# Layer 0's first projections: values ended ahead of keys, evacuations in order of need, another bank for the third unit

## The reference

```python
hx = modulate(rmsnorm(x_lat, g_attn[l]), sh1x, sc1x)
hc = modulate(rmsnorm(x_ctx, g_attn[l]), sh1c, sc1c)
aqx, akx, avx, bqx, bkx, bvx = split_cols(hx @ w_in[l])
aqc, akc, avc, bqc, bkc, bvc = split_cols(hc @ w_in[l])
qx, kx, vx = gqa_heads(aqx, akx, avx, g_qa[l], g_ka[l])   # per-head RMS norm of q and k
qx, kx = apply_rope(qx, cos, sin), apply_rope(kx, cos, sin)
```

## Time and profile before

| | before |
|---|---|
| three runs, us | 1725.15, 1731.41, 1724.01 (median 1725.15) |
| the profiled execution, us | 1729.36 |
| its span, us | 1727.6 |
| mean granted TensorE clock | 0.987 |
| busy share of the span | PE 95%, PE weight load 81%, DVE 64%, ACT 45%, POOL 36% |
| chain that ended last, by engine | PE 81%, DVE 9%, issue 4%, ACT 3%, POOL 2%, DMA 1% |

### The profile page before, as it was taken

One profiled execution on the slowest core, in us unless ns is written; L12 is line 12 of the kernel. 1 busy time (PEld: TensorE's weight loads), 2 busy tenths in 40 slices (PEclk: granted clock), 3 DMA queues, 4 the chain that ended last, 5 costly groups with the idle time before them and its releaser, 6 DMA issues.

```text
span 1727.6 us, 25951 instructions
## 1 busy us (share of the span) xinstructions
PE 1647.1 (95%) x9530; PEld 1395.6 (81%) x9530; DVE 1113.2 (64%) x1744; ACT 770.1 (45%) x1273; POOL 620.5 (36%) x316
## 2 busy tenths in 40 slices
PE   5899999889999999999999998999989999999997
PEld 3778887668888888888888876788767888888886
DVE  7877678868976576676245774778665763353256
ACT  6546666554443312332133344676564543243242
POOL 0356661110132233333332307664222254444442
PEclk9899999999999999999999999999999999999999
DMA  9430000025233343443334422001103133333232
GB/s 395 174 107 25 26 25 25 16 95 192 66 109 99 108 134 99 134 124 131 134 110 134 146 98 86 25 26 38 37 25 110 62 110 98 98 97 98 98 96 87
DMA packets 45533, 168.24 MB, mean 97 GB/s; under 512 B 4736, under 2 KB 6784, under 8 KB 43520
## 3 DMA queue, kind: packets, MB, share of 16 engines
q1 hardware_dynamic: 40896, 156.50, 27.2%
q10 hardware_dynamic: 4544, 10.49, 1.7%
HBM read 161.73 MB, written 5.24 MB: 97 GB/s over the span
## 4 chain that ended last, share of the span: by engine, by line
PE 81%; DVE 9%; issue 4%; ACT 3%; POOL 2%; DMA 1%; SPq 0%; DVEq 0%; ACTq 0%; POOLq 0%
PE ps L1270 23%; PE ps L1271 22%; PE ps L1272 22%; PE ps L1401 4%; PE ps L1415 4%; PE ps L1434 2%; PE ps L1435 1%; DVE junk_lead L2145 1%; DVE sqsum L2233 1%; DVE ht L2260 1%; DMA ada_first<-first_d 1%; DVE nb L2427 1%; DVE junk_mid L2163 1%; DMA w_raw<-w_d 1%; DVE pt_lo L2452 1%
## 5 line engine op out<-in xcount | busy, mean ns | idle before, releaser
L1146 POOL TENSOR_TENSOR w_lo<-w_raw,w_hi 128x1024 fp32r<-128x1024 f32 x175 | 441.6, 2526 | 927.8 <-ACT w_hi L1718 895.4
L1270 PE MATMUL ps<-h_hi,w_hi 128*128 128x512 f32 (+1 forms) x1592 | 568.9, 357 | 11.3 <-DVE h_lo L2268 8.3
L1271 PE MATMUL ps<-h_lo,w_hi 128*128 128x512 f32 (+1 forms) x1592 | 557.3, 350 | 0.0
L1272 PE MATMUL ps<-h_hi,w_lo 128*128 128x512 f32 (+1 forms) x1592 | 557.0, 350 | 0.0
L1270 PEld LDWEIGHTS ps<-h_hi,w_hi 128*128 128x128 f32 x1592 | 303.5, 191 | 60.2 <-issue 21.0
L1272 PEld LDWEIGHTS ps<-h_hi,w_lo 128*128 128x128 f32 x1592 | 303.0, 190 | 39.8
L1271 PEld LDWEIGHTS ps<-h_lo,w_hi 128*128 128x128 f32 x1592 | 303.6, 191 | 35.5
L1718 ACT ACTIVATE w_hi<-w_raw 128x1024 fp32r<-128x1024 f32 x188 | 198.4, 1056 | 232.3 <-PE ps L1272 213.8
L1270 PE MATMUL ps<-a_hi,w_hi 128*128 128x512 f32 (+1 forms) x552 | 191.6, 347 | 1.2 <-DVE a_lo L2642 1.2
L1271 PE MATMUL ps<-a_lo,w_hi 128*128 128x512 f32 (+1 forms) x552 | 191.3, 347 | 0.0
L1272 PE MATMUL ps<-a_hi,w_lo 128*128 128x512 f32 (+1 forms) x552 | 191.0, 346 | 0.0
(11 more groups left out here) (186 smaller groups left out, 2403.5 us busy)
## 6 DMA issues: line engine op xcount, KB each, us to landing
w_raw<-w_d SPq DMA_DIRECT2D x188, 512.0 KB, 3.5
ada_b<-ada_d SPq DMA_DIRECT2D x56, 512.0 KB, 4.4
ada_first<-first_d SPq DMA_DIRECT2D x8, 1024.0 KB, 20.2
ada_lead<-ada_d SPq DMA_DIRECT2D x14, 512.0 KB, 3.7
ada_mid<-ada_d SPq DMA_DIRECT2D x10, 512.0 KB, 8.7
x_sb<-x_d SPq DMA_DIRECT2D x2, 1536.0 KB, 8.8
x_sb<-x_d ACTq DMA_DIRECT2D x1, 3072.0 KB, 11.4
x_spill_d<-x_sb ACTq DMA_DIRECT2D x1, 2048.0 KB, 7.4
```

Of the source, the lines that this page charges most:

```text
L1146: nc.gpsimd.tensor_tensor(w_lo[:, c % RING, :], w_raw[:, c % RAW, :], w_hi[:, c % RING, :].bitcast(f32), ALU.subtract).then_inc(w_lo_done, 1)
L1270: nc.tensor.matmul(out, lh, rh, start=first, stop=False)
L1271: nc.tensor.matmul(out, lh, rl_, start=False, stop=False)
L1272: return nc.tensor.matmul(out, ll, rh, start=False, stop=last)
```

## The change

Four things, all in layer 0:

1. In the last slice (k 7) of the first two units PE takes unit 1 (values) ahead of unit 0 (keys). The list `first` is turned round accordingly, so that counts 1 and 2 of `proj_done` are the values' and 3 and 4 the keys'.
2. `unit_banks`: unit 2 goes to banks 2 and 0 (before 0 and 1), unit 3 to 1 and 2, unit 4 to 0 and 1, units 5 and 6 to 2 and 0. The values' turn goes through bank 1 (before bank 2).
3. `first_out` gives the six operations that read the first two units fixed places ahead of everything else on ACT: EV of the values' g 0, EV and SQ of the keys' g 0, EV of the values' g 1, EV and SQ of the keys' g 1.
4. The planner runs with this and gives other orders on ACT, POOL and DVE. PE's and SP's orders are as before but for the last slice and the banks.

```diff
@@ unit_banks
-        return {0: (0, 1), 1: (2, 3), 2: (0, 1), 3: (2, 0), 4: (1, 2), 5: (0, 1), 6: (0, 1)}.get(u, (7, 7))
+        return {0: (0, 1), 1: (2, 3), 2: (2, 0), 3: (1, 2), 4: (0, 1), 5: (2, 0), 6: (2, 0)}.get(u, (7, 7))
@@ mixing_plan
+    def first_out():
+
+        k, v = units[:FIRST_TILES]
+        for n, x in enumerate((v["EV"][0], k["EV"][0], k["SQ"][0], v["EV"][1], k["EV"][1], k["SQ"][1])):
+            x["pos"] = -30 + .1 * n
+
...
+    if l == 0:
+        first_out()
...
-    turn_values(v0, (2, 2) if l == 0 else (2, 3), 0)
+    turn_values(v0, (1, 1) if l == 0 else (2, 3), 0)
...
-    first = [p for x in units[:FIRST_TILES] for p in x["P"]]
+    first = [p for x in units[:FIRST_TILES][::-1] for p in x["P"]]
@@ first_tiles
-                    for y in units:
+                    for y in units[::-1] if k == KT - 1 else units:
```

## The result

The change made the kernel slower, clearly though by little: 1733.51 us in the median of 20 runs (1730.42 to 1735.91) against 1727.97 us in 20 runs of before (1723.64 to 1732.16), ratio 1.0029, 95% interval 1.0021 to 1.0036. That is 5.5 us more, where 1.9 us less was forecast, and above the range of 1719.8 to 1728.4. Of the 10.2 us between the forecast 1723.3 and the measured median, 2.8 lie in before itself, whose first three runs had a median of 1725.15. By the bound of 0.5% the ratio counts as no change. The profiled execution took 1732.62 us, its span is 1730.8 us, its mean clock 0.986.

What follows compares the result with a forecast made beforehand. It took DVE, not PE, to end the stretch near the start: PE gains 3.69 us, DVE only 1.60 + 0.27 = 1.87, the other terms nothing. So 1725.15 becomes 1723.3 us (0.11% faster), range 1719.8 to 1728.4.

Steps and rivals of the forecast that it cites:

- Pause and fall at 65 to 72 us: PE at unit 2's start: the pause goes (1.97 us) and the clock's fall at 68 us with it (1.72 us).
- The first shuffle: DVE's shuffle of the keys, forecast to start at 65.96 instead of 66.23, a gain of 0.27 us.
- the second at 74.23: DVE's shuffle of unit 2, forecast at 74.33 instead of 76.20, with the 1.60 us wait ahead of it gone.
- Unit 6's weights late on ACT: Raw load lands at 75.9, ACT stands 1.3 us; PE loses some 0.7 us, covered by its idle time at the turn.
- DVE, not PE, is what ends this stretch: From 76.2 to 105.1 us DVE is on the path, so PE's 3.69 us gain counts only as DVE's 1.87.
- the term for DVE: DVE up to the values' low part: gains 1.60 + 0.27 = 1.87 us, whatever PE gains.
- the shuffle of unit 3, now ahead of ada tile 23: DVE's new order was to change no time there, only needing unit 3's evacuation one tile sooner, at 82.9 us.
- Its low part: DVE's low part of the values' first piece, forecast to start at 102.43 instead of 104.30.
- that the gain reaches the end of the program: Rest of units 5 and 6, head factors and everything that follows were all to move by 1.87 us.
- one fall of the clock more or less: Allowance in the range for a short fall elsewhere in the program, 1.7 us each way.
- the idle time at the turn: PE waiting for DVE before the values' second piece: 1.6 to 2.3 us in place of 0.48.
- The second rival: The clock's fall moves to the values' turn, costing 1.72 us: -0.15 us in all, 1725.0 us; chance 0.20.

Runs made afterwards that it cites:

- p_act: The change with only ACT's fixed order (keys first); banks, turn's bank and last slice as before; 1727.23 us, ratio 0.9994 against before.
- a_gate: The change with the gate's two small DVE additions planned behind ada tile 29 instead of tile 23; 1727.91 us, ratio 1.0002 against before.
- b_hit: The kernel before with only the gate's additions moved, behind ada tile 24 instead of 23, onto POOL's split; 1734.93 us, ratio 1.0036 against before.
- a_both: The change with the gate's additions behind ada tile 29 and the values' first low part ahead of tiles 28 and 29; 1724.51 us, ratio 0.9981.
- after_3: The change itself, unaltered, timed once more against before on the same chip; 1733.27 us, ratio 1.0029.
- a_vl: The change with DVE taking the values' first low part ahead of ada tiles 28 and 29; 1725.76 us, ratio 0.9987 against before.
- both edits: Gate's additions behind ada tile 29, values' first low part ahead of tiles 28 and 29; ratios 0.9981 (change), 1.0002 (before), 0.9985 (ACT's order alone).

## Why the prediction was wrong

**Held.** Pause and fall at 65 to 72 us gone (3.7 us gained by PE at 75 us, 3.69 forecast). The first shuffle at 65.92 (65.96), the second at 74.23 without a wait (74.33). Unit 6's weights late on ACT: 75.27 (75.9), covered. DVE, not PE, is what ends this stretch. In p_act, where the pause is closed and DVE's list is as in before, PE's matmuls stand 1.9 us ahead of before at 200 us (early scatter of 0.4 us taken off), the forecast 1.87.

**Failed: the term for DVE.** The prediction said of the shuffle of unit 3, now ahead of ada tile 23, that "that changes no time on DVE", and so that DVE gains 1.87 us. It counted DVE's own work and never asked what the shuffle starts on POOL. The shuffle came 4.6 us sooner (87.17 to 82.54), and with it POOL's product, its sum and the split of unit 7's weights: 90.71 to 86.07. DVE's gate additions moved by only 2.1 us, from 87.80 to 85.69. Two things 2.5 us apart came to lie on each other, and DVE lost 2.43 us: 0.3 behind the sum, the rest behind the split. Its low part started at 104.62 instead of the forecast 102.43, later even than before's 104.30. a_gate shows the rest of the step nearly right: with the pair out of the way PE's matmuls stand 1.5 us ahead of before at 200 us (early scatter of 0.4 us taken off), against 1.87 forecast.

**Failed too: that the gain reaches the end of the program.** The prediction let all that follows move by 1.87 us and allowed for one fall of the clock more or less. a_gate and p_act have the early gain of 1.5 and 1.9 us, and their ratios are 1.0002 and 0.9994. In both profiles the fall at about 318 us takes more than that away. So with the meeting of the additions and POOL taken out the change is level with before, not 0.11% faster: the forecast ratio of 0.9989 lies outside a_gate's interval.

The rule was at hand. The Trainium skill (SBUF — State Buffer, SBUF: two separate sides) says that a DVE instruction with two SBUF inputs and a GpSimd instruction that reads SBUF take turns at a shared pair of ports, each holding it to its end. The trace agrees: the second addition is over 0.02 us after POOL's instruction, in the change, in b_hit and in a_both. Where the pair began first it was not held up: in both profiles of before, in a_gate and in p_act POOL's product starts 0.16 to 0.17 us before the pair is over, and the pair takes 0.35 to 0.36 us. The profile of before had a row of the loss as well. POOL ran from 128.63 to 130.10, and a low part that takes 0.95 us in the median of its eight rows took 1.95:

```profile
128.63 1.47 POOL L1192 TENSOR_TENSOR p_sb<-p_sb,ri 128x768 f32<-128x768 f32 x1 [8.96 <-DVE ri L2434]
128.96 1.95 DVE L2405 TENSOR_TENSOR kb_lo<-b_raw,kb_hi 128x768 fp32r<-128x768 f32 x1 [0.41 <-ACT kb_hi L1891]
```

**Failed in size: the idle time at the turn.** 4.49 us instead of 1.6 to 2.3. The second rival, that the clock's fall moves to the turn, came true as to place: in all three profiles of the change the clock is low for 3.4 us there, a cost of 1.7 us. But the rival had reckoned with a pause of 1.6 to 2.3 us, and the fall came by another, longer one. The length of a pause does not settle alone whether a fall follows: 1.80 to 1.81 us at 65 us was followed by a fall in four of four profiles, 1.43 us (a_gate) and 2.78 us (b_hit) at the turn were not.

**Not foreseen: the clock's part in the median.** Each run's record has its span and mean clock. Twice the missing share of the clock times the span is its time at 1.2 GHz; half of that, taken off, is a time nearly without falls. This is an estimate, with means over the runs. For before it gives 45.5 us at the low level and 1705.1 us; for the change 52.6 us and 1707.0 us; for a_gate 48.6 and 1703.6; for a_both 43.7 and 1702.9; for b_hit 56.6 and 1706.4. So of the change's 5.5 us some 1.9 are waits and some 3.5 are more time at the low level; after_3 and the runs of before beside it give 0.8 and 4.0, so the split is good to about 1 us. That the second part comes with the first was shown: b_hit, where the additions alone were moved, has both, and a_gate has less of both than the change. So has a_vl (43.9 and 1703.1, without one run whose recorded clock, 0.939, is far from all others). By which pauses of the later program it comes is open. The falls at 365, 1080 and 1240 us differ between profiles of one kernel; the one at 318 us did not in the five profiles of the two kernels. No run was made to tell that apart.

## What to carry to other kernels

Before moving an instruction, follow what it releases on the other engines, and lay the new times of DVE and GpSimd side by side: a DVE instruction of 0.2 us with two sources in SBUF that meets a running GpSimd instruction is over only when that one is, and the profile books it as busy. If an engine's queue is full right up to the point where PE needs one thing of it, gains of PE ahead of that point turn into idle time there; move that one thing forward in the queue first (a_vl, a_both), then close the pause. Keep small housekeeping instructions where nobody is due behind them.

## What was not expected of the hardware

The pair of additions of 128x8 elements took 0.35 to 0.37 us in the five profiles where no GpSimd instruction was running when it began. Where one was, it took 2.77 to 2.90 us in five profiles and 2.38 to 2.39 us in the three with both edits. And the clock's falls make two profiles of one kernel differ by up to 6.7 us of span (1725.4 to 1732.1 us for the change), more than the change is worth. A single profile places the causes, but the sign of 3 us needs the median of many runs.
